# Attention's gate units moved behind the recurrence, and nine pairs of gate units a layer by seven block products

## The reference

```python
z = rms_norm(x, norm_g) @ w_in      # split into the branches' inputs and gate_logits (3 * 1024)
y_rnn = (rg_lru(x_rnn, ...) * silu(g_rnn)) @ rg_out
y_sc  = (sc_b * causal_depthwise_conv(sc_c * x_sc, sc_conv_w) * silu(g_sc)) @ sc_out
y_att = (mla(c_q, c_kv, k_rope, ...) * silu(g_att)) @ mla_out
gates = sigmoid(gate_logits + gate_b)          # three gates of 1024 channels
merged = gates[0] * y_rnn + gates[1] * y_sc + gates[2] * y_att
return x + merged @ w_out
```

## Time and profile before

| | |
|---|---|
| median of 3 runs | 1704.94 us (1704.68 to 1708.34) |
| the profiled execution | 1704.46 us, its span 1702.5 us |
| PE busy, matmul / weight load | 99% / 92% of the span |
| POOL, DVE, ACT busy | 71%, 60%, 31% |
| PE's granted clock, mean | 0.999 |

### The profile page before, as it was taken

One profiled execution on the slowest core, in us unless ns is written; L12 is line 12 of the kernel. 1 busy time (PEld: TensorE's weight loads), 2 busy tenths in 40 slices (PEclk: granted clock), 3 DMA queues, 4 the chain that ended last, 5 costly groups with the idle time before them and its releaser, 6 DMA issues.

```text
span 1702.5 us, 31980 instructions
## 1 busy us (share of the span) xinstructions
PE 1682.9 (99%) x11720; PEld 1570.0 (92%) x11720; DVE 1020.2 (60%) x1439; ACT 522.8 (31%) x939; POOL 1210.9 (71%) x1349
## 2 busy tenths in 40 slices
PE   7999999999999999999999999999999999999999
PEld 7999999999999999999998888898888888888887
DVE  7966758485645454566358657484846445367651
ACT  5524333332322331123135233333323313312320
POOL 7764748485688777677866748484857898785784
PEclk9999999999999999999999999999999999999999
DMA  4421212122232233222532312221222222322233
GB/s 154 147 98 63 97 68 90 57 93 86 88 111 74 86 111 113 74 82 94 186 117 76 111 62 93 73 98 61 92 100 76 99 95 86 141 87 73 99 125 126
DMA packets 49411, 164.21 MB, mean 96 GB/s; under 512 B 6048, under 2 KB 7456, under 8 KB 49056
## 3 DMA queue, kind: packets, MB, share of 16 engines
q1 hardware_dynamic: 41328, 146.56, 25.7%
q10 hardware_dynamic: 8032, 17.00, 2.9%
HBM read 152.21 MB, written 10.81 MB: 96 GB/s over the span
## 4 chain that ended last, share of the span: by engine, by line
PE 83%; DVE 9%; issue 3%; DMA 2%; POOL 1%; ACT 1%; ACTq 0%; DVEq 0%; SPq 0%; POOLq 0%
PE slots L567 71%; PE slots L632 3%; PE slots L844 3%; PE slots L666 3%; PE slots L650 1%; PE slots L728 1%; DVE early L1418 1%; DMA w_raw<-w_units 1%; POOL w_lo L527 1%; DVE early L1433 1%; DVE qr_hi_and_lo L1250 1%; DVE kr_lo L1250 1%; DVE kn_lo L1250 1%; PE slots L601 1%; DMA residual_or_merged<-xt 0%
## 5 line engine op out<-in xcount | busy, mean ns | idle before, releaser
L457 POOL TENSOR_TENSOR w_lo<-w_raw,w_hi 128x256 fp32r<-128x256 f32 x940 | 805.9, 887 | 19.6
L452 POOL TENSOR_SCALAR w_hi<-w_raw 128x1024 fp32r<-128x1024 f32 x235 | 275.0, 1170 | 282.7 <-PE slots L567 252.8
L567 PE MATMUL slots<-h_hi,w_hi 128*128 128x264 f32 (+1 forms) x1920 | 469.8, 310 | 1.0 <-DVE sc_pad L1546 1.0
L567 PE MATMUL slots<-h_lo,w_hi 128*128 128x264 f32 (+1 forms) x1920 | 464.5, 307 | 0.0
L567 PE MATMUL slots<-h_hi,w_lo 128*128 128x264 f32 (+1 forms) x1920 | 463.9, 307 | 0.0
L567 PEld LDWEIGHTS slots<-h_hi,w_hi 128*128 128x128 f32 x1920 | 311.1, 189 | 18.5 <-issue 2.0
L567 PEld LDWEIGHTS slots<-h_hi,w_lo 128*128 128x128 f32 x1920 | 310.2, 189 | 16.2
L567 PEld LDWEIGHTS slots<-h_lo,w_hi 128*128 128x128 f32 x1920 | 310.5, 188 | 15.4
L567 PE MATMUL slots<-branch_hi,w_hi 128*128 128x264 f32 (+1 forms) x552 | 143.9, 320 | 10.5 <-DVE branch_lo L1263 8.9
L567 PE MATMUL slots<-branch_lo,w_hi 128*128 128x264 f32 (+1 forms) x552 | 142.3, 317 | 0.0
L567 PE MATMUL slots<-branch_hi,w_lo 128*128 128x264 f32 (+1 forms) x552 | 141.8, 316 | 0.0
(11 more groups left out here) (274 smaller groups left out, 3289.7 us busy)
## 6 DMA issues: line engine op xcount, KB each, us to landing
w_raw<-w_units SPq DMA_DIRECT2D x251, 512.0 KB, 3.3
stream<-sc_acc ACTq DMA_DIRECT2D x16, 264.0 KB, 2.1
sc_back<-stream SPq DMA_DIRECT2D x2, 2112.0 KB, 8.1
x_old<-stream SPq DMA_DIRECT2D x16, 264.0 KB, 4.5
stream<-residual_or_merged ACTq DMA_DIRECT2D x16, 264.0 KB, 2.4
ab_raw<-w_units SPq DMA_DIRECT2D x8, 512.0 KB, 4.1
residual_or_merged<-xt ACTq DMA_DIRECT2D x4, 528.0 KB, 7.7
stream<-xt ACTq DMA_DIRECT2D x1, 2112.0 KB, 9.3
```

Source lines behind the costliest of these rows:

```text
L452: pool.tensor_scalar(hi, raw, 1.0, 1.0, ALU.mult, ALU.mult).then_inc(sem("hi_part"), 1)
L457: op = pool.tensor_tensor(lo[:, cols], raw[:, cols], hi[:, cols].bitcast(F32), ALU.subtract)
L567: mm = pe.matmul(out[:, a_, 0:t1 - t0], w(k), x(k)[:, t0:t1], start=(n == 0), stop=(n == 3 * ks - 1))
```

## The change

The stage tables: RG has six units a turn (attention's gates are gone from it), MR has six (they stand there as "a"), and gate pairs number 0 to 11 in PE's order: a and g of each MR turn, then those of MS. The first three (`PLAIN`) are dense, the other nine go by `seven`; before, the four of MS did.

```diff
-STAGES = {..., "RG": (4, 8, 0), "MR": (4, 4, 0), "MS": (4, 4, 0), ...}
+PLAIN = 3
+PAIR_LIST = [("MR", i, n, j) for i in range(4) for n, j in (("a", 0), ("g", 3))] + [("MS", i, "g", 0) for i in range(4)]
+STAGES = {..., "RG": (4, 6, 0), "MR": (4, 6, 0), "MS": (4, 4, 0), ...}
```

```diff
-                with pe.Fori(0, 4) as i:
-                        dense("MR", l, i, f"g{n}", n, h_hi, h_lo, None, l == DEPTH - 1)
-                        dense("MR", l, i, f"y{n}", 2 + n, x_hi, x_lo, None if n else tile_there, l == DEPTH - 1)
+                for i in range(4):
+                    for n in range(2):
+                        gate_pair(2 * i + n)
+                        dense("MR", l, i, f"y{n}", 2 + 3 * n, y2_hi, y2_lo,
+                              None if n else (lambda k: at("rnn_lo", l, k // 2, k % 2 + 1)), l == DEPTH - 1, range(KT), 2 + n)
```

```diff
+                def branch_lower(i):
+                    for n in range(2):
+                        pool.wait_ge(*at("scb_hi", l, i, n + 1))
+                        pool.tensor_tensor(tile(y_lo, i * 2 + n), sc_back[:, i % 2 * 2 + n, :],
+                                           tile(y_hi, i * 2 + n).bitcast(F32), ALU.subtract).then_inc(sem("scb_lo"), 1)
+                split_pair(0)
+                for i in range(4):
+                    split_unit("MR", l, i, 2, 2)
+                    split_pair(2 * i + 1)
+                    split_unit("MR", l, i, 5, 3)
+                    split_pair(2 * i + 2)
+                    branch_lower(i)
```

```diff
+                def att_gate(i):
+                    for n in range(2):
+                        dve.wait_ge(*was_read("RG", l, 3, "my1"))
+                        dve.wait_ge(*gate_there(2 * i, n))
+                        dve.scalar_tensor_tensor(kept(l, tile(xm, i * 2 + n)), kept(l, g_t[n][:]), 1.0,
+                                                 kept(l, tile(xm, i * 2 + n)), ALU.add, ALU.mult)...
+                for p in range(PLAIN, 8):
+                    i = p // 2
+                    if p % 2 == 0:
+                        merge("MR", i - 1, 1)
+                    for n in range(3):
+                        sum_lower(p - PLAIN, n)
+                    gate_sums(p - PLAIN)
+                    weight_sums(p - PLAIN + 1)
+                    if p % 2 == 0:
+                        att_gate(i)
+                    else:
+                        merge("MR", i, 0)
```

More of the change, by code:

```diff
@@ L816, in _, with seven @@
                     for n in range(2):
-                        dense("RG", l, i, f"mg{n}", 4 + n, h_hi, h_lo, None, l == DEPTH - 1)
-                    for n in range(2):
-                        dense("RG", l, i, f"my{n}", 6 + n, y_hi, y_lo,
-                              None if n else (lambda k: at("att_lo", l, k // 2, k % 2 + 1)), l == DEPTH - 1)
-                merge("MR", y2_hi, y2_lo, lambda k: at("rnn_lo", l, k // 2, k % 2 + 1))
-                def seven(i):
+                        dense("RG", l, i, f"my{n}", 4 + n, y_hi, y_lo,
+                              None if n else (lambda k: at("att_lo", l, k // 2, k % 2 + 1)), l == DEPTH - 1, range(KT),
+                              (2 * half + n) % RING)
+                with pe.Fori(0, 2) as two:
+                    for half in range(2):
+                        recurrent(two * 2 + half, half)
+                def seven(stage, i, name, q, ahead=0):
                     w = SIDES[l]
@@ L1165, in _ @@
                         act.activation(tt[s][:], tt[s][:], ACT.Sqrt, scale=0.25).then_inc(sem("root"), 1)
-                    gates("RG", i, "mg", "my", GB2)
+                    for n in range(2):
+                        act.wait_ge(*ready("RG", l, i, f"my{n}"))
+                        act.activation(kept_halves(l, tile(xm, i * 2 + n)), kept_slot(l, n), ACT.Copy).then_inc(
+                            freed("RG", f"my{n}"), 1)
                     for s in range(2):
@@ L1205, in keep_part, with open_gates @@
                         sem("part_kept"), 1)
+                def open_gates(q):
+                    stage, i, name, j = PAIR_LIST[q + PLAIN]
+                    which = GB1 if stage == "MS" else GB2 if name == "a" else GB0
+                    for n in range(2):
+                        if n == 0:
+                            act.wait_ge(*at("gate_sum", l, q, 5))
+                        else:
+                            act.wait_ge(*was_read(stage, l, i, f"{name}0"))
+                            act.wait_ge(*was_read(stage, l, i, f"{name}1"))
+                        act.activation(kept(l, g_t[n][:]), kept(l, g_t[n][:]), ACT.Tanh, bias=param(l, which, i * 2 + n),
+                                       scale=(0.5, -0.5)[n]).then_inc(sem("gate_open"), 1)
@@ L1794, in _ @@
-                third(3)
-                weight_sums(0)
-                merge("MR", 3, "y", "g", "R", range(1, 2))
+                mixes(0)
+                mixes(1)
+                att_gate(0)
+                mixes_lower(0)
+                mixes_lower(1)
+                mixes(2)
+                merge("MR", 0, 0)
+                mixes_lower(2)
+                merge("MR", 0, 1)
+                mixes(3)
+                weight_sums(0)
+                mixes_lower(3)
+                att_gate(1)
@@ new lines, in _ @@
+                for p in range(PLAIN, 8):
+                    i = p // 2
[5 more added lines that the diff above has]
+                    weight_sums(p - PLAIN + 1)
+                    if p % 2 == 0:
+                        att_gate(i)
+                    else:
+                        merge("MR", i, 0)
+                merge("MR", 3, 1)
```

327 lines of the change are left out of this document (185 added, 142 removed), and 6 rows, old and new, of tables (SIGNALS, TILES).

## The result

The change takes 1710.9 us (median of 8 runs, 1705.1 to 1715.9) against 1705.9 us before (8 runs beside it): ratio 1.0029, 95% interval 1.0016 to 1.0041. It is slower by 0.29%, where the prediction had 1696.8 us and a chance of 0.75 for faster. The profiled execution took 1710.13 us.

What follows compares the result with a forecast made beforehand. PE's instruction stream was taken to bound the kernel, with POOL's loop setting MR's pace after the change. 1704.46 − 12.75 (matmuls) − 6.8 (old waits) + 11.9 (new waits) = 1696.8 us, range 1690 to 1706.

Steps and rivals of the forecast that it cites:

- The matmuls, 12.75 us off: PE: five more pairs a layer by seven products save 1.52 us each in layer 0, 1.03 in layer 1.
- The old waits, 6.8 us, go: Entry of MS: PE's waits in the first two pairs of each layer, 6.8 us in all, disappear.
- RG with six units, and the mixes, at 0: RG's shorter PE turns keep 3.9 us of slack, and DVE's four mixes fit before pair 3: no cost.
- Rival C: RG: six-unit turns expose the recurrence; each us late beyond 3.9 costs six times, 2 us over gives 1709; chance 0.06.
- The first handover, 7.4 us after pair 2: MR: both raw buffers freed after a tanh (0.7), a high part (0.6) and seven low pieces at 0.88 us.
- The five loops, 83.2 us: MR: POOL's load, split and low-part loop sets the pace: three with y1 at 16.3 us, two with y0 at 17.15.
- late by some 0.5 us at each a pair: MR, optimistic bound: two merges before DVE's lower parts delay each a pair, costing about 1.5 us a layer.
- MS's first y unit at 99.4 us after pair 2: First handover, five loops and last leg reach it at 99.4 us; PE without waits at 96.4 and 93.9.
- MS's second pair, 1.7 us a layer: MS starts without slack, so its second pair still waits for DVE's recombination, 1.7 us a layer.
- New waits: PE waits for POOL's loop, 3.0 and 5.5 us by layer, plus 1.7 a layer in MS: 11.9 in all.
- Rival B: MR: POOL and DVE hinder each other throughout; 1712.8 us at contended lengths, 1710.4 if never running at once; chance 0.13.

Runs made afterwards that it cites:

- the move alone: The change with all eight MR pairs kept dense, only MS's four by seven products: 1702.7 us, ratio to before 0.9970 to 0.9988.
- e1: The change with DVE's second merge in even pairs moved between the second and third recombination: 1710.5 us, ratio to before 1.0016 to 1.0034.
- e2: The change with POOL's short-conv branch low part in four pieces of 132 columns a tile: 1715.7 us, ratio to before 1.0038 to 1.0065.
- e7: The change with POOL's short-conv low parts spread one by one behind the y units' splits: 1703.0 us, ratio to before 0.9972 to 0.9990.
- e11: e9 plus MR's y units and the pair's second unit loaded, split and handed over in halves: 1692.7 us, ratio to before 0.9916 to 0.9941.
- e3: The change with POOL's short-conv branch low part computed for only one column a tile: 1698.5 us, ratio to before 0.9945 to 0.9971.
- e4: The same kernel as the move alone (the change with MR's pairs all dense): 1702.7 us, ratio to before 0.9970 to 0.9988.
- e13: The change with only the loads and splits in halves added: 1705.7 us, ratio to before 0.9990 to 1.0008.
- e5: The change with POOL's short-conv branch low part moved behind the next y0 split: 1704.2 us, ratio to before 0.9983 to 1.0003.
- e8: The change with DVE's first recombination of each pair ahead of the third lower part: 1706.6 us, ratio to before 0.9996 to 1.0015.
- e9: The change with second merge late, first recombination early and short-conv low parts spread behind y splits: 1701.3 us, ratio to before 0.9960 to 0.9981.
- e10: e9 with half of the y units' low part on POOL left out in MR turns 1 to 3: 1688.6 us, ratio to before 0.9887 to 0.9916.
- e12: e4 with DVE's first recombination ahead of the third lower part: 1699.4 us, ratio to before 0.9950 to 0.9976.

## Why the prediction was wrong, by its steps

- **The matmuls, 12.75 us off**: right. Free pairs take 10.22 and 9.88 us, dense units of MS kept 5.86 and 5.56. The layer-1 pair is even 0.2 shorter than I took.
- **The old waits, 6.8 us, go**: in the move alone pair 8 is at 10.22 and 10.33 us. In the change it has 3.8 and 3.2 us over the free pace, new ones.
- **RG with six units, and the mixes, at 0**: right. A turn is 41.08 us, PE waits nowhere in it, and from RG's start to the end of pair 2 the change has no wait. Rival C is out.
- **The first handover, 7.4 us after pair 2**: wrong, 9.0 (648.8 − 639.76) and 10.1. I took POOL's low pieces at 0.88 us; the six rows

```profile
641.26 6.61 POOL L550 TENSOR_TENSOR w_lo<-w_raw,w_hi 128x256 fp32r<-128x256 f32 x6 [5.57 <-ACT w_hi L1258]
```
```profile
1478.31 7.47 POOL L550 TENSOR_TENSOR w_lo<-w_raw,w_hi 128x256 fp32r<-128x256 f32 x6 [3.67 <-ACT w_hi L1258]
```

  are 1.10 and 1.25 us a piece, since DVE's weight sums and mixes run beside just these.
- **The five loops, 83.2 us**: 86.0 and 86.1. A loop with y1 is 16.1 to 16.8 where the forecast had 16.3, but for one; one with y0 is 17.7 to 19.1, not 17.15. The split behind branch_lo, which I took as clean at 4.0, is 1.49 + 3.57 = 5.1 us, since DVE, held up by branch_lo, is late and now adds beside the split. Two loops also have a slow load, the last with y1 in layer 0 (18.0 in all) and the second with y0 in layer 1: 5.0 us from the issue of the pair's second unit to the first work on it (724.91 to 729.94), 3.5 to 3.6 elsewhere. Why is open.
- **DVE "late by some 0.5 us at each a pair"**, in the bounds only, and hidden under the loop in the sum: PE waits for it 1.6 to 2.7 us at each even pair, at block 4 and in all but one at the first recombination. I had the two merges, but not that their additions and the three lower parts would stand beside POOL's longest instructions.
- **MS's first y unit at 99.4 us after pair 2**: 105.9 and 106.6. POOL had it split at 104.1 and 105.2, so 4.7 and 5.8 us of the error are the loop's own terms; PE came 1.8 and 1.4 us later still, late from pair 8's waits for DVE and, in layer 0, the clock.
- **MS's second pair, 1.7 us a layer**: 0.0 and 2.1.

**The step that failed** is the price of DVE and POOL side by side. The forecast took it as a mean (0.88 us a piece), as nothing (the split behind branch_lo at 4.0) or as hidden (DVE's 0.5 us), and it measured 1.10 to 1.25, 5.1, and 1.6 to 2.7. The mechanism, a loop that sets the pace, was right, but DVE's lateness is a second limit close to it, and the larger doesn't hide the smaller.

New waits were forecast at 4.7 and 7.2 us; the pairs of the trace and the y units behind them have 10.0 and 14.6 over the forecast's paces. That is 12.7 us more, and RG to MS is indeed 12.3 us over what the forecast implies (782.2 against 777.5 − 7.7 = 769.9).

Rival B had the right engines and nearly the right time (1710.4 to 1712.8), and its point of decision, loops of 17.3 us, was nearly met: 86.05 / 5 = 17.2. Its extent was not: the splits of y1 and most of POOL's pieces ran at their clean length. That its time comes so close is in part luck, since 1.7 us of the change's profiled time is the clock in MR, of which B says nothing.

I gave it 0.13, because a DVE addition beside POOL takes 1.2 us there, less than the 1.43 of taking turns. That was misread. The 1.2 is taking turns: in the trace of before, from 640 us on, each of the 46 additions (and lower parts) of 512 columns that begin beside a 256-column instruction of POOL ends 0.55 us after it, whatever its own length, and the 6 beside a 1024-column one 0.53 to 0.54. An addition takes 0.69 alone, so its first 0.14 us or so pass while POOL still runs. How long it takes then goes by the length of POOL's instruction: 0.95 beside 132 columns, 1.2 beside 256, 1.52 beside 1024, 1.79 beside 528. The Trainium skill has the rule (SBUF — State Buffer, "Who interferes with whom"): the port pair that the two engines share is "an exclusive lock", and a DVE instruction with two SBUF inputs contends with a GpSimd instruction that reads SBUF. This trace agrees, with the ends above. I had weighed the rule by a mean over short instructions.

## What to carry to other kernels

When a ring of steps (load, split, load, sum, low part) feeds an engine, add its legs and compare with the engine's stretch before asking who is named in the list of waits: the one named is the last to arrive, and taking it away (e1, e2) may only change the name. Put work of the ring's engine where it waits for a load anyway (e7), and shorten legs that stand one behind the other by halving what is handed over (e11).

Two limits that lie within a few per cent hide each other: one edit alone took off 0 to 8 of the 16 us. And a contention price taken from a row holds for the instruction lengths of that row alone. Look at when the two instructions end, not at how long one takes: that shows whether they take turns.

## What the runs showed of the hardware

**DVE and POOL take turns.** From 640 us on, a DVE addition or subtraction of 512 or 528 columns with both inputs in SBUF (weight sums, lower parts, merges) that begins beside a split, a low part or a branch_lo of POOL ends 0.53 to 0.57 us after it. It is so in all 61 cases of the trace of before and in 101 of 103 of the change. Turns cost POOL as well: its branch_lo of 528 columns takes 1.32 us and, begun beside an addition, 1.75.

**The clock behind a wait.** In the change, around pair 8 of layer 0 (length, busy times, clock, as above):

```profile
736.50:741.00 4.50, 2.65 (x16) 2.44 (x16) 4.50 (x4) 0.34 (x1) 4.42 (x4) 0.84 0.54 220
741.00:745.61 4.61, 4.61 (x32) 4.38 (x31) 2.09 (x4) 0.00 (x0) 4.53 (x6) 0.79 0.18 18
```

PE is busy for 2.65 of 4.50 us, and in and behind this stretch part of the time is granted at the lower level (1.2 GHz). That costs about 0.16 x 4.50 + 0.21 x 4.61 = 1.7 us (an estimate) on top of a wait of 1.8, and the pair is 3.8 us over the free pace: this wait cost twice its length. In MR and MS the clock was low once in the change, e3, e4 and e13, twice in e5 and three times in e2, each time in or right behind a single wait of PE of 1.8 to 2.5 us. Not every such wait brings it: e1 has one of 2.5 and e7 one of 1.9, and their clock stays at the upper level from RG to MS, as it does before and in e8, e9, e10, e11 and e12.

Such stretches, each worth some 1.7 us, also come in stages that the change doesn't touch, from none to two ahead of RG in a trace, and they widen the runs: the change's eight go from 1705.1 us at a mean granted 1.000 to 1715.9 at 0.993. With each run's lost share of the clock taken off (an estimate, from a mean of three digits), the medians are 1702.9 before, 1705.6 for the change, 1707.8 for e1, 1703.1 for e8, 1708.3 for e2, 1697.7 for e7, 1698.5 for e9, 1700.7 for e13 and 1691.4 for e11. The main findings stay: slower than before, e1 and e2 no gain, e11 the fastest with nothing left out. But only 2.7 us of the change's 5.0 and 2.7 of e2's 4.8 are left.
